# Dilated window attention inside a matmul stream: visits of two pairs of blocks in place of visits of one

## The chip, the cores and the metric

The kernel runs on one core of a Trainium2 chip, in one launch. The metric is the device time of that launch in microseconds (us), the median of several runs. The same work must be done before and after; only its order, its buffers and its waits differ.

## What is computed

The reference is one layer of a decoder trunk over 2048 tokens of width 1024, all in fp32. Cut to what matters here:

```python
h = x * (1.0 + scale) + shift
proj = h @ w_in + b_in        # 1024 -> 8704 columns: q, k, v | z_attn | u_x, g_b, g_c, z_conv | g_A, g_B
for g, (window, dilation) in enumerate(((128, 1), (512, 4), (2048, 16))):
    o_g, lse_g = dilated_window_attention(q_g, k_g, v_g)   # 4 heads of 64 per group, ALiBi bias
o_attn = sum over groups of softmax(lse)_g * o_g
y_attn = (o_attn * silu(z_attn)) @ w_proj_attn
y_conv = (g_b * conv3(g_c * u_x) * silu(z_conv)) @ w_proj_conv
merged = sigmoid(g_A) * y_attn + sigmoid(g_B) * y_conv
x = layer_norm(alpha * x + gate * (merged @ w_out + b_out))
```

Attention is done in blocks of 128 queries of one residue class. A block of group 0 or 1 sees its own 128 keys and, unless it is the first of its class, the 128 before; a block of group 2 sees its own alone. There are 6 tiles `t` (two heads each) of 16 blocks, 96 blocks in all. Of a block the kernel needs the scores, their maximum with the bias, the exponentials and their sum, the probabilities turned round (transposed), and their product with the values.

## The kernel before

**The product stream.** The input projection is a two-level block product in the manner of Strassen and Winograd: for each group of weight tiles (`PLAN`, 68 groups) seven products `p` = 0 to 6 are made of halves of the token axis and of the contraction. Products are numbered n = 7g + p, and this number is the clock of the whole kernel: every engine has its own loop over `m` and each piece of work hangs on some `m`. I call it the slot. A product (`product`, lines 1189 to 1234) is twelve matmuls of 512 columns, four each of high by high (L1224), high by low (L1229) and low by high parts (L1232), since fp32 operands are split in two rounded parts. Slots 14 to 475 are the projection, then come 32 units of the two output projections of the branches (L1356 to L1386), then slots 476 to 531 for the last matmul.

**Banks.** PSUM has eight banks. The four of `acc` serve the products (`bank`, L515): p = 0, 2, 4, 6 of a group build up in one bank on top of each other, `acc[g % 2]`; p = 1 and 5 in another, p = 3 in a third. The sums in between have to be read out before the next product is added on top. So in `product` p = 2 waits until p = 0 has been copied to `part` (semaphore `p1_out`), p = 4 waits for the copy of p = 2 (`u2_out`), p = 6 for the read of p = 4 (`c22_out`). In each of these three only one other product lies between.

**ScalarE (ACT)** in its iteration m (L1636 to L1690, in this order): takes product m-1 where its p is 0, 1 or 2 (`take`, L1505), or p = 6 of the q, k, v and gate groups (`take`, L1509 and L1514), or computes the sigmoid of p = 6 in a `gz` group (`conv_sigmoid(g, 1)`, L1539, which waits for `c12_out`); then the exponentials of a visit (`soften`, L1570, one activation for each of two blocks and two heads); then the copies of turned probabilities (`copy_probs`, L1580); then rounds the weights of slot m+4 (`round_w`, L1488); then, of slot m-2, the sigmoids of the gate groups (L1521), of p = 4 of `gz` (`conv_sigmoid(g, 0)`, L1535) and the first tap of the convolution of `ug` (`first_tap`, L1547). Sigmoid and Exp don't lie in the same table: between them an ACT_TABLE_LOAD runs.

**VectorE (DVE)** in its iteration m: takes product m-1 where its p is 3 to 6, then `take_o` (L1972, attention outputs from PSUM), then `bias_max` (L1961, one tensor_tensor_reduce for each block and head, then L1965), then `combine` (sums of weight tiles), then `split_w` of slot m+3. Most of these go through one helper, L1719.

**Order of groups.** Slots 14 to 62 and 63 to 125 make q, k, v (groups 0 to 17). Groups 18 to 33 alternate `ug` (even) and `gz` (odd), 34 is `za`, 35 to 42 are `gate` (slots 245 to 300). Group 43 (slot 301) is `za` again, 44 to 59 alternate `ug` and `gz`, 60 to 67 are `gate`. In `gz` VectorE's p = 5 step multiplies the convolution's second half by two factors, one of them the sigmoid of ScalarE, before it raises `c12_out`; product p = 1 of the next group and `conv_sigmoid(g, 1)` wait for that.

**Visits.** Attention goes in between the products. `TWO_AT` holds the slots of 48 visits, one for each pair of blocks j: 119, 125 and so on every 6 slots to 287, then 307 to 421. After product n of a visit TensorE multiplies the previous pair's values (`weigh_values`, L1322) and then makes this pair's scores (`scores`, L1289). ScalarE softens at m = n+2, TensorE turns the probabilities after product n+3 (`turn_probs`, L1305), ScalarE copies them at m = n+4. One set of buffers: scores in two banks (`sc_ps`), turned probabilities in `po` and `xb`, outputs in half of `xb`, one `prob` in SBUF.

```python
TURN_P = [at + 3 for at in TWO_AT[:NTWO]]
                    if m - 2 in TWO_AT[:NTWO]:        # ScalarE
                        soften(TWO_AT.index(m - 2))
                    if m - 1 in TWO_AT[:NTWO]:        # VectorE
                        bias_max(TWO_AT.index(m - 1))
```

Of the kernel before, what the change touches and what calls it, by code (L numbers as in the profile page):

```python
# [11 lines left out]
P = 128  # L12
# [122 lines left out]
ATT0 = FIRST[1] + 8 * NP  # L135
NSTEP = NPAIR * NBLK
PAUSE = (FIRST[2] - 9, FIRST[2] + 6)
# [11 lines left out]
SUM_AT = [at + 1 for at in TWO_AT if at >= BG2 + 16][:2]  # L149
# [32 lines left out]
def att_loads(j):  # L182

    return sum({0: 32, NTWO: 16}.get(i, 48) for i in range(j % 2, j + 1, 2))
# [15 lines left out]
def build(nc, x, x_t, c, w_ada_t, w_gate, b_ada, cols_h, w_first, w_tiles, w_pa, w_pc, w_out, b_out, ln_g, ln_b, out):  # L200
# [22 lines left out]
    with ExitStack() as top:  # L223
# [59 lines left out]
        o_ps = xb[:, 0:2 * P]  # L283
# [29 lines left out]
        q_two = view(A, 2, P)  # L313

        k_two = view(A + 256, 3, P)
        v_two = view(A + 640, 3, P)
        dist = view(A + 1024, 2, P)
        bm = view(A + 1280, 2, 2 * P)

        prob = view(A + 1792, 2, 4 * P)  # L320
        prob_t = view(A + 1792, 2, 4 * P)
# [8 lines left out]
        za_s = view(0, 4, CH)  # L330
# [108 lines left out]
        att_in = [sem(f"att_in{r}") for r in range(2)]  # L439
# [213 lines left out]
        with nc.Block() as block:  # L653
            @block.sync
            def _(sp):
# [48 lines left out]
                def load_t(ph, p):  # L704
                    if p == 0:
                        if ph == 1:
                            for idx in (0, 2, 3):
                                sp.wait_ge(hk_out[idx], 16 * KH)
                            sp.wait_ge(tk_out, 16 * 4 * KH)
                        if ph == 2:  # L710
                            for n in ("b11", "b21", "b22", "t1", "t2", "t3", "rest"):
                                sp.wait_ge(dumped[n], 16)
                            sp.wait_ge(gb_out, 16)
                            sp.wait_ge(za_out, 64)
                            for r in range(2):
                                sp.wait_ge(wos_out[r], 16 * 4)
# [7 lines left out]
                def load_att(j):  # L724
                    if j:

                        t, blk = blocks_of(j - 1)
                        first = 0 if has_prev(t, blk) else 1
                        sp.wait_ge(pv_done, j - 1)
                        sp.dma_start(v_two[:, first:3], vt_d[t, blk + first - 1:blk + 2].rearrange("b i f -> i b f")).then_inc(  # L730
                            att_in[j % 2], 16)
                    if j == NTWO:
                        return
# [10 lines left out]
                    if j:  # L744
                        sp.wait_ge(scored, j)
                    first = 0 if has_prev(t, blk) else 1
                    sp.dma_start(q_two.rearrange("p a i -> p (a i)"), qk_d[0, t, :, blk * P:(blk + 2) * P]).then_inc(att_in[j % 2], 16)
                    sp.dma_start(k_two[:, first:3].rearrange("p a i -> p (a i)"),
                                 qk_d[1, t, :, (blk + first - 1) * P:(blk + 2) * P]).then_inc(att_in[j % 2], 16)
# [166 lines left out]
                for m in range(NPAIRED, NS):  # L916
# [9 lines left out]
                    if m + 3 in TWO_AT:  # L926
                        load_att(TWO_AT.index(m + 3))
# [66 lines left out]
            def _(pool):  # L994
# [90 lines left out]
                def store_za(g, n):  # L1085
# [4 lines left out]
                    pool.dma_start(za_d[tile, :, tok], za_s[:, n]).then_inc(za_out, 16)  # L1090
# [25 lines left out]
                for m in range(NPAIRED, NS + 2):  # L1116
# [21 lines left out]
                    if m - 2 in TWO_AT[1:]:  # L1138
                        store_att(TWO_AT.index(m - 2) - 1)
# [42 lines left out]
            def _(pe):  # L1182
# [5 lines left out]
                def product(n):  # L1188
# [6 lines left out]
                    if n in (NS, NS + 1, NS + 3, NS + NP):  # L1195
                        pe.wait_ge(conv_gated, M0 + 4 + {NS: 1, NS + 1: 3, NS + 3: 4, NS + NP: 2}[n])
                    if p == 0:
                        if g >= NG + 2:
                            pe.wait_ge(c21_dve, c21_count(NG - 1, False) + g - NG - 1)
                        elif PLAN[g - 2].kind in C21_ACT:  # L1200
                            pe.wait_ge(c21_act, c21_count(g - 2, True))
                        else:
                            pe.wait_ge(c21_dve, c21_count(g - 2, False))
                        if g == 2:
                            pe.wait_ge(c11_out, 1)
                    if p == 1:
                        pe.wait_ge(c12_out, g)
                    if p == 2:
# [71 lines left out]
                def scores(j):  # L1280
                    t, blk = blocks_of(j)
                    pe.wait_ge(att_in[j % 2], att_loads(j))
                    if j:
                        pe.wait_ge(max_ready, j)
                    for h in range(2):
                        rows_h = slice(h * HEAD, (h + 1) * HEAD)
                        for s in range(2):
                            keys = k_two[rows_h, s:s + 2].rearrange("p a i -> p (a i)") if has_prev(t, blk + s) else k_two[rows_h, s + 1]
                            mm = nc.tensor.matmul(sc_ps[:, h, columns(j, s)], q_two[rows_h, s], keys, start=True, stop=True)  # L1289
                    mm.then_inc(scored, 1)  # L1290

                def turn_probs(j):
                    t, blk = blocks_of(j)
                    pe.wait_ge(exp_done, j + 1)
                    if j:
                        pe.wait_ge(pt_ready, j)
                        pe.wait_ge(o_ready, j)
                    else:
                        pe.wait_ge(v_copied, 4 * len(VG))
                    if TURN_P[j] > SUM_AT[0]:  # L1300
                        pe.wait_ge(gbc_done, sum(TURN_P[j] > at for at in SUM_AT))
                    for s in range(2):
                        for h in range(2):
                            for half in range(0 if has_prev(t, blk + s) else 1, 2):
                                tr = nc.tensor.transpose((po, xb)[s][:, (2 * h + half) * P:(2 * h + half + 1) * P],  # L1305
                                                         prob[:, h, (2 * s + half) * P:(2 * s + half + 1) * P], ident[:])
                    tr.then_inc(turned, 1)

                def weighed(slot):

                    return sum(at <= slot for at in TWO_AT[1:])

                def weigh_values(j):
                    t, blk = blocks_of(j)
                    pe.wait_ge(att_in[(j + 1) % 2], att_loads(j + 1))
                    pe.wait_ge(pt_ready, j + 1)
                    for s in range(2):
                        first = 0 if has_prev(t, blk + s) else 1
                        for h in range(2):
                            cols_h = slice(h * HEAD, (h + 1) * HEAD)  # L1320
                            for half in range(first, 2):
                                mm = nc.tensor.matmul(o_ps[cols_h, s * P:(s + 1) * P], v_two[:, s + half, cols_h],  # L1322
                                                      prob_t[:, s, (2 * h + half) * P:(2 * h + half + 1) * P],
# [3 lines left out]
                def sum_gate(half):  # L1327
# [4 lines left out]
                    nc.tensor.matmul(xb[:], ones[:], gate_acc[:, half * CH:(half + 1) * CH],  # L1332
# [59 lines left out]
                for n in range(NPAIRED, NS):  # L1392
# [3 lines left out]
                    if n in TWO_AT:  # L1396
                        j = TWO_AT.index(n)
                        if j:
# [17 lines left out]
            def _(act):  # L1416
# [106 lines left out]
                def za_sigmoid(g, n):  # L1523
                    sc = PLAN[g].sc
                    if n < 3:
                        act.wait_ge(z1_ready, kind_count(g, "gz") + 3 * sc + n + 1)
                        nc.scalar.activation(za_s[:, n], tmp[:, n], ACT.Sigmoid).then_inc(sig_ready, 1)
# [824 lines left out]
```

## Time and profile before

| what | value |
|---|---|
| median of three runs | 1857.41 us (1857.31 to 1858.83) |
| time of the profiled execution | 1858.69 us |
| its span in the profile | 1856.9 us |
| mean granted TensorE clock | 0.995 |
| TensorE (PE) busy | 1829.5 us, 99% |
| VectorE (DVE) busy | 1241.1 us, 67% |
| ScalarE (ACT) busy | 861.9 us, 46% |
| GpSimd (POOL) busy | 200.5 us, 11% |
| chain that ended last | PE 93%, DMA 2%, DVE 2%, ACT 1%, issue 1% |
| exponentials, L1570 | 192 activations 86.4 us, reads of the sum 35.9 us, 25 table loads 32.1 us |

The span is 1.8 us shorter than the execution's own time; the rest is start and end. A busy time is the union of an engine's instructions. Matmuls overlap each other in the profile, so the steps from one start to the next tell the pace better than durations. An engine's idle time stands in brackets with what released it.

### The profile page before, as it was taken

What the parts mean: (1) busy time and instruction counts of PE and PEld (TensorE: products, weight loads), DVE (VectorE), ACT (ScalarE), POOL (GpSimd) and SP (SyncE); (2) the same over time, 40 slices, a digit from 0 to 9 for tenths busy, and PEclk for the clock granted to TensorE, in tenths of its full rate; (3) what the DMA queues carried; (4) which work ended last, traced back from release to release, by engine and by line L of the source; (5) the groups of instructions that cost most, each with busy time, mean ns of one, the idle gap of its engine ahead of it and who ended that gap; (6) DMA issues with size and microseconds to landing.
All of it is one profiled execution on the core that took longest, in us unless ns stands there. A gap on an engine that the chain in (4) does not pass through costs nothing.

```text
span 1856.9 us, 24751 instructions
## 1 busy us (share of the span) xinstructions
PE 1829.5 (99%) x8783; PEld 1490.7 (80%) x8783; DVE 1241.1 (67%) x2185; ACT 861.9 (46%) x1552; POOL 200.5 (11%) x326
## 2 busy tenths in 40 slices
PE   8999999999999999999999999999999999999997
PEld 7788888888888888877878888888888888887885
DVE  8755744456666666665686666766677576647987
ACT  5544633444555545666665455455444410014342
POOL 0232111100000000011200000000111100011110
PEclk9999999999999999999999999999999999999999
DMA  9876532432232322364862222222396778879782
GB/s 374 291 241 239 188 130 93 117 112 81 94 111 67 109 92 88 129 215 143 299 237 91 94 99 103 80 91 80 118 293 198 257 234 229 249 219 295 206 233 85
DMA packets 161916, 311.27 MB, mean 168 GB/s; under 512 B 35745, under 2 KB 87713, under 8 KB 157570
## 3 DMA queue, kind: packets, MB, share of 16 engines
q1 hardware_dynamic: 132786, 208.64, 34.8%
q0 software_dynamic: 28720, 100.46, 15.8%
q8 instruction: 71, 1.16, 0.3%
q10 hardware_dynamic: 288, 0.59, 0.1%
q14 instruction: 51, 0.42, 0.1%
HBM read 217.06 MB, written 92.57 MB: 167 GB/s over the span
## 4 chain that ended last, share of the span: by engine, by line
PE 93%; DMA 2%; DVE 2%; ACT 1%; issue 1%; SPq 0%; POOL 0%; ACTq 0%; DVEq 0%
PE acc L1224 24%; PE acc L1229 24%; PE acc L1232 24%; PE acc L1378 3%; PE acc L1386 3%; PE acc L1382 3%; PE score L1289 2%; PE xb L1322 2%; PE acc L1240 1%; PE xb L1305 1%; PE pt_o L1305 1%; DMA room<-in_x 1%; DMA vt_d<-room 1%; DVE room L1719 1%; DMA room<-gb_d 1%
## 5 line engine op out<-in xcount | busy, mean ns | idle before, releaser
L1224 PE MATMUL acc<-t_hi,w_hi 128*128 128x512 f32 x1888 | 519.7, 397 | 3.5 <-DVE room L1719 2.2
L1229 PE MATMUL acc<-t_lo,w_hi 128*128 128x512 f32 x1888 | 505.9, 390 | 0.0
L1232 PE MATMUL acc<-t_hi,w_lo 128*128 128x512 f32 x1888 | 505.3, 389 | 0.0
L1229 PEld LDWEIGHTS acc<-t_lo,w_hi 128*128 128x128 f32 x1888 | 354.4, 188 | 75.8
L1232 PEld LDWEIGHTS acc<-t_hi,w_lo 128*128 128x128 f32 x1888 | 354.4, 188 | 75.0
L1224 PEld LDWEIGHTS acc<-t_hi,w_hi 128*128 128x128 f32 x1888 | 344.4, 188 | 84.7 <-issue 14.3
L1719 DVE TENSOR_TENSOR room<-acc,part 128x512 f32<-128x512 f32 x198 | 136.7, 691 | 216.1 <-PE acc L1232 214.4
L1505 ACT ACTIVATE part<-acc,cols 128x512 f32<-128x512 f32 x198 | 136.3, 688 | 211.3 <-PE acc L1232 211.0
L1719 DVE TENSOR_TENSOR w_lo<-w_raw,w_hi 128x512 fp32r<-128x512 f32 x278 | 187.7, 686 | 38.0 <-ACT w_hi L1488 36.6
L1488 ACT CAST w_hi<-w_raw 128x512 fp32r<-128x512 f32 x270 | 166.2, 616 | 99.4 <-PE acc L1232 97.0
L1488 ACT CAST w_hi<-s_tmp 128x512 fp32r<-128x512 f32 x203 | 125.6, 619 | 170.3 <-PE acc L1232 152.5
L1719 DVE TENSOR_TENSOR w_lo<-s_tmp,w_hi 128x512 fp32r<-128x512 f32 x203 | 139.4, 687 | 66.2 <-ACT w_hi L1488 63.8
L1719 DVE TENSOR_TENSOR room<-room 128x512 f32<-128x512 f32 (+2 forms) x208 | 145.4, 703 | 39.0 <-ACT room L1535 30.6
L1570 ACT ACTIVATE room<-room 128x128 f32<-128x128 f32 (+1 forms) x192 | 86.4, 451 | 54.8 <-DVE room L1965 54.6
L1076 POOL DMA_DIRECT2D att_d<-room x48 | 34.4, 717 | 528.7 <-DVE room L1972 528.7
L1719 DVE TENSOR_TENSOR w_raw<-w_raw 128x512 f32<-128x512 f32 x98 | 67.5, 688 | 4.6
L1719 DVE TENSOR_TENSOR s_tmp<-w_raw,s_tmp 128x512 f32<-128x512 f32 x74 | 51.0, 690 | 28.9 <-PE acc L1232 25.9
L1961 DVE CUSTOM_DVE_ANT_0 room<-score,room 128x128 f32<-128x128 f32 (+1 forms) x192 | 58.7, 362 | 16.8 <-PE score L1289 16.5
L1719 DVE TENSOR_TENSOR t_lo<-t_raw,t_hi 128x2048 fp32r<-128x2048 f32 (+1 forms) x29 | 57.6, 1993 | 13.9 <-ACT t_hi L1597 10.2
L1589 ACT CAST t_hi<-t_raw 128x2048 fp32r<-128x2048 f32 x6 | 11.4, 1907 | 112.7 <-DMA t_raw<-conv_d 112.7
L1098 POOL DMA_DIRECT2D gate_d<-room x64 | 34.8, 545 | 239.7 <-ACT room L1521 239.6
L1719 DVE TENSOR_TENSOR s_tmp<-w_raw 128x512 f32<-128x512 f32 x74 | 51.0, 689 | 5.4 <-DMA w_raw<-mix_d 1.1
(257 smaller groups left out, 2087.2 us busy)
## 6 DMA issues: line engine op xcount, KB each, us to landing
w_raw<-in_w_tiles SPq DMA_DIRECT2D x132, 512.0 KB, 4.4
gate_d<-room POOLq DMA_DIRECT2D x64, 256.0 KB, 4.0
qk_d<-room POOLq DMA_DIRECT2D x24, 512.0 KB, 5.1
w_raw<-gate_d SPq DMA_DIRECT2D x24, 512.0 KB, 6.1
room<-qk_d SPq DMA_DIRECT2D x74, 128.0 KB, 3.0
t_raw<-tr_d SPq DMA_DIRECT2D x8, 1024.0 KB, 6.9
conv_d<-room POOLq DMA_DIRECT2D x16, 512.0 KB, 2.9
w_raw<-mix_d SPq DMA_DIRECT2D x16, 512.0 KB, 7.0
```

The lines of the kernel that those rows point to most:

```text
L1224: nc.tensor.matmul(to, hi_w[:, k], hi_t[:, k], start=(first and k == 0), stop=False, skip_group_check=True)
L1229: nc.tensor.matmul(to, hi_w[:, k], lo_t[:, k], start=False, stop=False, skip_group_check=True)
L1232: mm = nc.tensor.matmul(to, lo_w[:, k], hi_t[:, k], start=False, stop=(last and k == KH - 1), skip_group_check=True)
L1289: mm = nc.tensor.matmul(sc_ps[:, h, columns(j, s)], q_two[rows_h, s], keys, start=True, stop=True)
L1378: nc.tensor.matmul(to, w_h[:, k], b_half(True, k), start=(k == 0), stop=False)
L1382: nc.tensor.matmul(to, w_l[:, k], b_half(True, k), start=False, stop=False)
L1386: mm = nc.tensor.matmul(to, w_h[:, k], b_half(False, k), start=False, stop=(k == KT - 1))
L1488: nc.scalar.copy(w_slot(hi_parts, n), src).then_inc(hi_done, 1)
L1505: ins = nc.scalar.activation(to, src, ACT.Identity, bias=col(gr.tb if p == 1 else gr.ta))
L1570: ex = nc.scalar.activation(prob[:, h, o], prob[:, h, o], ACT.Exp, bias=all_m[:, t, h, b], scale=SCALE, accum_out=all_d[:, t, h, b])
L1719: return nc.vector.tensor_tensor(o, a, b, op)
L1961: own_t.up(nc.vector.tensor_tensor_reduce(out=prob[:, h, o], in0=sc_ps[:, h, o], in1=bm[:, h, o.start - 2 * P * s:2 * P], scale=1.0, scala ...
```

## The change

Two pairs of blocks go in one visit, so there are 24 visits (`SCORE_AT`), 35/3 slots apart up to number 13 and 11 apart from number 14 on: 129, 140, 152, 164, 175, 187, 199, 210, 222, 234, 245, 257, 269, 280, then 307, 318, 329, 340, 351, 362, 373, 384, 395, 406. The values are multiplied at the next visit's slot, those of the last before the break at 290 and the very last at 417. ScalarE softens both pairs at m = n+4, TensorE turns both after product n+6, VectorE finds both pairs' maxima at m = n+2. The second pair needs buffers of its own: scores and turned probabilities of a pair share two banks (`att_ps`), the outputs take the fourth bank of `acc`, and so the products get by with three. q, k, v and `prob` are doubled in SBUF, in room that `za_s` and others gave up. In the diff a few lines on addresses, on loads of v and on `za_s` are left out.

```diff
-ATT0 = FIRST[1] + 8 * NP
-PAUSE = (FIRST[2] - 9, FIRST[2] + 6)
-TWO_AT = []
-for j in range(NTWO + 1):
-    slot = TWO_AT[-1] + 6 if j else ATT0
-    TWO_AT.append(PAUSE[1] if PAUSE[0] <= slot < PAUSE[1] else slot)
-TURN_P = [at + 3 for at in TWO_AT[:NTWO]]
-ATT_END = TWO_AT[-1]
+NVISIT = NTWO // 2
+VISIT0 = FIRST[1] + 66
+BREAK = 14
+SCORE_AT = [VISIT0 + 35 * v // 3 if v < BREAK else FIRST[2] + 6 + 11 * (v - BREAK) for v in range(NVISIT)]
+TURN_P = [at + 6 for at in SCORE_AT]
+WEIGH_AT = [SCORE_AT[v + 1] if v + 1 not in (BREAK, NVISIT) else at + (10 if v + 1 == BREAK else 11) for v, at in enumerate(SCORE_AT)]
+ATT_END = WEIGH_AT[-1]
...
-        o_ps = xb[:, 0:2 * P]
+        o_ps = acc[:, 3]
+        att_ps = ((sc_ps[:, 0], sc_ps[:, 1]), (po[:], xb[:]))
...
+        prob = (view(0, 2, 4 * P), view(2 * CH, 2, 4 * P))
+        prob_t = prob
...
         def bank(g, p):
-            if p in (0, 2, 4, 6):
-                return acc[:, g % 2]
-            return acc[:, 2] if p in (1, 5) else acc[:, 3]
+            if p in (1, 5):
+                return acc[:, 1]
+            return acc[:, 2 * ((g + (p == 3)) % 2)]
...
                             sp.wait_ge(za_out, 64)
+                            sp.wait_ge(pv_done, 2 * BREAK)
...
                     if p == 0:
-                        if g >= NG + 2:
-                            pe.wait_ge(c21_dve, c21_count(NG - 1, False) + g - NG - 1)
-                        elif PLAN[g - 2].kind in C21_ACT:
-                            pe.wait_ge(c21_act, c21_count(g - 2, True))
-                        else:
-                            pe.wait_ge(c21_dve, c21_count(g - 2, False))
-                        if g == 2:
-                            pe.wait_ge(c11_out, 1)
+                        pe.wait_ge(c11_out, 1 if g == 2 else g)
...
                     if p == 3:
-                        pe.wait_ge(c11_out, g)
-                        if g == 2:
-                            pe.wait_ge(c22_out, 1)
+                        if g > NG:
+                            pe.wait_ge(c21_dve, c21_count(NG - 1, False) + g - NG)
+                        elif PLAN[g - 1].kind in C21_ACT:
+                            pe.wait_ge(c21_act, c21_count(g - 1, True))
+                        else:
+                            pe.wait_ge(c21_dve, c21_count(g - 1, False))
...
                 def scores(j):
                     t, blk = blocks_of(j)
-                    pe.wait_ge(att_in[j % 2], att_loads(j))
-                    if j:
-                        pe.wait_ge(max_ready, j)
+                    u = j % 2
+                    if u == 0:
+                        pe.wait_ge(qk_in, 64 * (j // 2 + 1))
+                        if j:
+                            pe.wait_ge(pt_ready, j)
+                        else:
+                            pe.wait_ge(v_copied, 4 * len(VG))
...
-                    if n in TWO_AT:
-                        j = TWO_AT.index(n)
-                        if j:
-                            weigh_values(j - 1)
-                        if j < NTWO:
+                    if n in WEIGH_AT:
+                        for j in pair(WEIGH_AT.index(n)):
+                            weigh_values(j)
+                    if n in SCORE_AT:
+                        for j in pair(SCORE_AT.index(n)):
                             scores(j)
                     if n in TURN_P:
-                        turn_probs(TURN_P.index(n))
+                        for j in pair(TURN_P.index(n)):
+                            turn_probs(j)
...
-                    if m - 2 in TWO_AT[:NTWO]:
-                        soften(TWO_AT.index(m - 2))
+                    if m - 4 in SCORE_AT:
+                        for j in pair(SCORE_AT.index(m - 4)):
+                            soften(j)
                     if m - 1 in TURN_P:
-                        copy_probs(TURN_P.index(m - 1))
+                        for j in pair(TURN_P.index(m - 1)):
+                            copy_probs(j)
...
-                    if m - 1 in TWO_AT[1:]:
-                        take_o(TWO_AT.index(m - 1) - 1)
-                    if m - 1 in TWO_AT[:NTWO]:
-                        bias_max(TWO_AT.index(m - 1))
+                    if m - 1 in WEIGH_AT:
+                        for j in pair(WEIGH_AT.index(m - 1)):
+                            take_o(j)
+                    if m - 2 in SCORE_AT:
+                        for j in pair(SCORE_AT.index(m - 2)):
+                            bias_max(j)
```

## Rows read from the trace of the kernel before

**Rows 1.** The page, part 1: busy time and share of the span

```profile
PE 1829.5 (99%) x8783; PEld 1490.7 (80%) x8783; DVE 1241.1 (67%) x2185; ACT 861.9 (46%) x1552; POOL 200.5 (11%) x326
```

**Rows 2.** Waits, TensorE: us in total, times, longest us

```profile
PE acc L1224 <- ACT part L1505: 1.1, 1, 1.1
```

**Rows 3.** Timeline of TensorE around the visit at slot 161: start, us, instructions

```profile
499.46 0.39 PE L1232 MATMUL acc<-t_hi,w_lo 128*128 128x512 f32 x1
499.77 1.14 PE L1322 MATMUL xb<-room 128*64 128x128 f32 x16
...
500.65 0.27 PE L1322 MATMUL xb<-room 128*64 128x128 f32 x1
500.85 0.49 PE L1289 MATMUL score<-room 64*128 64x256 f32 x2
...
501.17 0.60 PE L1289 MATMUL score<-room 64*128 64x256 f32 x4
501.38 0.60 PE L1289 MATMUL score<-room 64*128 64x256 f32 x4
...
501.92 1.19 PE L1224 MATMUL acc<-t_hi,w_hi 128*128 128x512 f32 x4
502.95 1.08 PE L1229 MATMUL acc<-t_lo,w_hi 128*128 128x512 f32 x4
```

**Rows 4.** Timeline of TensorE, slots 259 to 261: the one wait for ScalarE

```profile
815.29 1.07 PE L1224 MATMUL acc<-t_hi,w_hi 128*128 128x512 f32 x4
...
818.01 1.07 PE L1224 MATMUL acc<-t_hi,w_hi 128*128 128x512 f32 x4
...
820.73 0.60 PE L1305 MATMUL pt_o<-ident,room 128*128 128x128 f32 x4
...
822.83 1.15 PE L1224 MATMUL acc<-t_hi,w_hi 128*128 128x512 f32 x4 [1.06 <-ACT part L1505]
```

**Rows 5.** Timeline of ScalarE in the same stretch

```profile
815.49 0.69 ACT L1514 ACTIVATE room<-acc,cols 128x512 f32<-128x512 f32 x1 [3.69 <-PE acc L1232]
816.28 1.28 ACT L1570 ACT_TABLE_LOAD   x1
817.57 0.51 ACT L1570 ACTIVATE room<-room 128x256 f32<-128x256 f32 x1
...
819.56 0.60 ACT L1488 CAST w_hi<-w_raw 128x512 fp32r<-128x512 f32 x1
...
822.01 0.67 ACT L1505 ACTIVATE part<-acc,cols 128x512 f32<-128x512 f32 x1
```

**Rows 6.** Timeline of ScalarE, slots 161 to 171: first tap, sigmoids, exponentials of a pair

```profile
500.98 1.15 ACT L1547 ACTIVATE room<-room,cols 128x1024 f32<-128x1024 f32 x1
...
520.93 0.69 ACT L1539 ACTIVATE room<-acc,cols 128x512 f32<-128x512 f32 x1 [1.54 <-DVE room L1719]
...
524.36 0.69 ACT L1505 ACTIVATE part<-acc,cols 128x512 f32<-128x512 f32 x1 [2.24 <-PE acc L1232]
525.07 1.28 ACT L1570 ACT_TABLE_LOAD   x1
526.37 0.40 ACT L1570 ACTIVATE room<-room 128x128 f32<-128x128 f32 x1
...
528.13 0.60 ACT L1488 CAST w_hi<-s_tmp 128x512 fp32r<-128x512 f32 x1
528.64 0.68 ACT L1505 ACTIVATE part<-acc,cols 128x512 f32<-128x512 f32 x1
```

**Rows 7.** Timeline of VectorE, slots 161 to 167: maxima of a pair, then a gz group

```profile
502.05 0.43 DVE L1961 CUSTOM_DVE_ANT_0 room<-score,room 128x256 f32<-128x256 f32 x1 [0.67 <-PE score L1289]
...
503.63 0.69 DVE L1719 TENSOR_TENSOR w_lo<-w_raw,w_hi 128x512 fp32r<-128x512 f32 x1
...
514.04 0.69 DVE L1719 TENSOR_TENSOR room<-acc,part 128x512 f32<-128x512 f32 x1 [0.92 <-PE acc L1232]
514.88 0.69 DVE L1719 TENSOR_TENSOR w_raw<-w_raw 128x512 f32<-128x512 f32 x1
...
519.41 1.42 DVE L1719 TENSOR_TENSOR room<-room 128x512 f32<-128x512 f32 x2 [1.23 <-ACT room L1535]
```

**Rows 8.** Timeline of TensorE in the last matmul, after a longer wait

```profile
1705.41 2.04 PE L1224 MATMUL acc<-w_hi,t_hi 128*128 128x512 f32 x4 [2.34 <-DVE sums_y L2109]
...
1709.71 1.08 PE L1224 MATMUL acc<-t_hi 128*128 128x512 f32 x4
```

**Rows 9.** Stretches: busy of PE, PEld, DVE, ACT, POOL, then PEclk, DMA share, GB/s

```profile
820.00:830.00 10.00, 8.94 (x44) 7.32 (x44) 6.47 (x9) 7.05 (x12) 1.80 (x3) 1.00 0.48 162
1705.00:1709.00 4.00, 3.59 (x9) 2.87 (x10) 2.88 (x8) 1.55 (x3) 1.76 (x3) 0.57 1.17 286
```

More of the change, by code:

```diff
@@ L179, in columns, with pair @@
     return slice(2 * P * s + (0 if has_prev(t, blk + s) else P), 2 * P * (s + 1))
-def att_loads(j):
-    return sum({0: 32, NTWO: 16}.get(i, 48) for i in range(j % 2, j + 1, 2))
+def pair(v):
+    return 2 * v, 2 * v + 1
 class Tally:
@@ L312, in build @@
         A = 2048
[L313 to L321, printed above, removed]
+        q_two = view(A, 2, 2, P)
+        k_two = view(A + 512, 2, 3, P)
+        v_two = view(A + 1280, 2, 3, P)
+        dist = view(A + 2048, 2, P)
+        bm = view(A + 2304, 2, 2 * P)
+        prob = (view(0, 2, 4 * P), view(2 * CH, 2, 4 * P))
+        prob_t = prob
         att_o = view(A + 2816, 2, 2 * P)
@@ L329, in build @@
         tmp3 = view(ROOM - 4 * CH, CH)
-        za_s = view(0, 4, CH)
+        za_s = [view(first, CH) for first in (6916, 6916 + CH, 8964, 8964 + CH)]
         gate_w = view(5888, 2, D)
@@ L438, in build @@
         dist_done = sem("dist_done")
-        att_in = [sem(f"att_in{r}") for r in range(2)]
+        qk_in = sem("qk_in")
+        v_in = sem("v_in")
         scored = sem("scored")
@@ L722, in load_t, with load_qk @@
                     sp.dma_start(dst, tr_d[(0, 1, 0)[ph], p]).then_inc(t_in[p % 4], 16)
-                def load_att(j):
-                    if j:
[L727 to L733, printed above, removed]
+                def load_qk(j):
                     t, blk = blocks_of(j)
@@ L925, in _ @@
                                 load_t(ph, p)
-                    if m + 3 in TWO_AT:
-                        load_att(TWO_AT.index(m + 3))
+                    if m + 4 in SCORE_AT:
+                        for j in pair(SCORE_AT.index(m + 4)):
+                            load_qk(j)
+                    if m - 2 in SCORE_AT:
+                        for j in pair(SCORE_AT.index(m - 2)):
+                            load_v(j)
                     for k in range(KT + 1):
@@ L1137, in _ @@
                         make_dist()
-                    if m - 2 in TWO_AT[1:]:
-                        store_att(TWO_AT.index(m - 2) - 1)
+                    if m - 2 in WEIGH_AT:
+                        for j in pair(WEIGH_AT.index(m - 2)):
+                            store_att(j)
                     if m == BG2 + 29:
@@ L1293, in turn_probs @@
                     t, blk = blocks_of(j)
+                    u = j % 2
                     pe.wait_ge(exp_done, j + 1)
[L1295 to L1301, printed above, removed]
                     for s in range(2):
@@ L1304, in turn_probs @@
                             for half in range(0 if has_prev(t, blk + s) else 1, 2):
-                                tr = nc.tensor.transpose((po, xb)[s][:, (2 * h + half) * P:(2 * h + half + 1) * P],
-                                                         prob[:, h, (2 * s + half) * P:(2 * s + half + 1) * P], ident[:])
+                                tr = nc.tensor.transpose(att_ps[u][s][:, (2 * h + half) * P:(2 * h + half + 1) * P],
+                                                         prob[u][:, h, (2 * s + half) * P:(2 * s + half + 1) * P], ident[:])
                     tr.then_inc(turned, 1)
                 def weighed(slot):
-                    return sum(at <= slot for at in TWO_AT[1:])
+                    return 2 * sum(at <= slot for at in WEIGH_AT)
                 def weigh_values(j):
                     t, blk = blocks_of(j)
-                    pe.wait_ge(att_in[(j + 1) % 2], att_loads(j + 1))
+                    u = j % 2
+                    if u == 0:
+                        pe.wait_ge(v_in, 32 * (j // 2 + 1))
+                        if j:
+                            pe.wait_ge(o_ready, j)
+                        if WEIGH_AT[j // 2] > SUM_AT[0]:
+                            pe.wait_ge(gbc_done, 2)
                     pe.wait_ge(pt_ready, j + 1)
@@ L1331, in sum_gate @@
                     pe.wait_ge(o_ready, weighed(SUM_AT[half]))
-                    nc.tensor.matmul(xb[:], ones[:], gate_acc[:, half * CH:(half + 1) * CH],
+                    nc.tensor.matmul(o_ps, ones[:], gate_acc[:, half * CH:(half + 1) * CH],
                                      start=True, stop=True).then_inc(gsum, 1)
@@ L1578, in copy_probs @@
                         first = 0 if has_prev(t, blk + s) else P
-                        to = prob_t[:, s].rearrange("p (h n) -> p h n", h=2)
-                        ins = nc.scalar.copy(to[:, :, first:], (po, xb)[s][:].rearrange("p (h n) -> p h n", h=2)[:, :, first:])
+                        to = prob_t[j % 2][:, s].rearrange("p (h n) -> p h n", h=2)
+                        ins = nc.scalar.copy(to[:, :, first:], att_ps[j % 2][s].rearrange("p (h n) -> p h n", h=2)[:, :, first:])
                     ins.then_inc(pt_ready, 1)
@@ L1910, in take_za @@
                         dve.wait_ge(sig_ready, sig + 4)
-                        nc.vector.scalar_tensor_tensor(out=za_s[:, 3], in0=bank(g, 6), scalar=col(gr.tb), in1=za_s[:, 3],
+                        nc.vector.scalar_tensor_tensor(out=za_s[3], in0=bank(g, 6), scalar=col(gr.tb), in1=za_s[3],
                                                        op0=ALU.add, op1=ALU.mult).then_inc(c21_dve, 1)
@@ L1961, in bias_max @@
                             own_t.up(nc.vector.tensor_tensor_reduce(
-                                out=prob[:, h, o], in0=sc_ps[:, h, o], in1=bm[:, h, o.start - 2 * P * s:2 * P], scale=1.0,
+                                out=prob[j % 2][:, h, o], in0=att_ps[j % 2][h][:, o], in1=bm[:, h, o.start - 2 * P * s:2 * P], scale=1.0,
                                 scalar=-3.0e38, op0=ALU.add, op1=ALU.max, accum_out=all_m[:, t, h, blk + s:blk + s + 1]))
```

62 lines of the change are left out of this document (39 added, 23 removed).

## The prediction

> **What bounds the kernel now.** I read the page's busy times first: TensorE is busy for 99% of the span, VectorE for 67%, ScalarE for 46% [rows 1]. So only two things can move the end: what TensorE executes, and the time in which it is made to wait. The view of waits says that in the whole product stream ScalarE made it wait once, for 1.1 us [rows 2]. Then I read the timeline of TensorE through one visit, to see what a visit costs beyond its matmuls [rows 3], and the timelines of ScalarE and VectorE where a visit falls on a product whose bank must be read at once [rows 4 to 7].
>
> **The pace.** A product takes 2.72 us, 815.29 to 818.01 [rows 4], 0.227 us a matmul. ScalarE's copy starts 0.20 us after its product ends (815.29 to 815.49), and TensorE goes on 0.15 us after that copy ends (822.01 + 0.67 = 822.68, then 822.83) [rows 4, 5]. p = 2 adds on p = 0 with one product between, p = 4 on p = 2 likewise. So from the end of the product that is read before, ScalarE's work up to the copy's end has 5.44 us less 0.15.
>
> **Part 1, half the visits: a gain.** In the visit at slot 161 the last product matmul starts at 499.46 and the values at 499.77: 0.31 instead of 0.23, 0.08 lost. The values' records step by 0.06 (499.77 to 500.65 is 15 steps of 0.88), but the step to the scores is 0.20: 0.14 lost. Scores go in pairs of records: 0.32 for the first pair, 0.21 for the second, 0.54 for the last two with the way out, against 0.21 a pair: 0.11 and 0.12 lost. The first four product matmuls take 1.03 instead of 0.91 [rows 3]: 0.12. That is 0.57, say 0.6 us, in each visit whatever its size. 24 visits less give 14.4 us; the break now separates values and scores at one more place, which takes 0.2 back: **-14.2 us**. Turning probabilities has almost no such cost (eight transposes in the 0.9 us that they take at any place); I take 0, between 0 and -1. The matmuls themselves are the same.
>
> **Part 2, both pairs' exponentials in one step: a cost.** ScalarE needs 1.99 us for a full pair (817.57 to 819.56) [rows 5], 1.76 where one block has no predecessor (526.37 to 528.13) [rows 6], so some 1.53 where both have none. One pair, with its table load, between two copies takes 4.96 us, start of the first to end of the second (524.36 to 528.64 + 0.68) [rows 6]. With 0.20 and 0.15 around it that is 5.3 of 5.44 us: it just fits. A second pair doesn't. Softening is at m = n+4, behind the copy of product n+3 and ahead of that of n+4, so it bites where n+4 has p = 0 or 2.
> - n with p = 5 (152, 187, 222, 257, 362; n+4 is p = 2): 4.96 + 0.23 + 1.99 + 0.35 = 7.5 us for two full pairs, 2.1 over; 1.9 with a mixed pair (257), about 1.2 with pairs of group 2 (362). At 152, 187, 222 VectorE makes it worse: its two maxima (1.58 us each, 502.05 to 503.63 [rows 7], 3.2 together) stand behind its work on p = 6, done about 2.3 us after that product, and ahead of the `combine` (0.6) that the rounding just before ScalarE's copy of p = 1 needs. That rounding ends at 2.3 + 3.2 + 0.6 + 0.5 = 6.6 instead of by 5.64: 1.0 more, 3.1 each. Together 3 x 3.1 + 1.9 + 1.2 = 12.4 us.
> - n with p = 3 in a `gz` group (164, 234, 318; n+4 is p = 0): before the exponentials stands the sigmoid that waits for VectorE's `c12_out`. VectorE reads p = 4 and goes on 0.84 later (514.04, 514.88 [rows 7]), then 3.2 of maxima, 1.2 for two helper steps, then four steps for p = 5, 2.8: 8.3 after p = 4 ends, which is 2.9 after p = 6. In rows 6 the sigmoid starts at 520.93, about 1.6 after p = 6. From it again 7.2, and 0.15: 10.3 against 5.44, 4.8 over; 4.3 with a mixed pair. Together 13.4.
> - n with p = 3 in a `gate` group (269): here the trace shows the case itself with one pair. From the end of p = 6 to the start of p = 2 it takes 7.54 us (815.29 to 822.83 [rows 4, 5]); a second, mixed pair makes 9.3: 3.9 over.
> - smaller: 340 (n+4 is p = 1, but exponentials, rounding and the first tap of 1.15 [rows 6] reach the copy of p = 2) 0.8, and 373, where the maxima stand ahead of the read of p = 4, 0.4.
> The sum is 12.4 + 13.4 + 3.9 + 1.2 = **+30.9 us**. Elsewhere the copy comes before the exponentials, or none is due; `ug` groups with n at p = 3 have no step of ScalarE that waits for p = 6, so they start early. The wait of rows 4 goes: the transposes' start to 822.83 is 2.1 us where 0.9 is needed, **-1.2**.
>
> By the Trainium skill, ScalarE: Activation LUTs, What ACT_TABLE_LOAD costs, a switch is the load of 1.283 us and a drain of about 1.38. The rows show the load at 816.28 and the first exponential at 817.57, so no drain here [rows 5]. With the drain ten of the chains above would be an estimated 14 us longer; the row excludes it, so it gets no chance of its own.
>
> **Part 3, the clock.** After the 2.34 us wait the next twelve matmuls took 4.30 us instead of 2.72 [rows 8], and the granted clock of that stretch is 0.57, the lower level of 1.2 GHz in most of it, where the stretch after a 1.06 us wait keeps 1.00 [rows 9]. The three of 3.1, the three of `gz` and the gate one are longer than 2.34: 7 x 1.6 = **+11.2 us**. Bounds: nothing, and twice that.
>
> **Part 4, what costs nothing.** Three banks for the products: p = 3 now waits for p = 6 of the group before, p = 0 for p = 3, with three products (8.2 us) between, more than any chain above; bound 0 to +2. Copies of two pairs stand behind the copies of products: 0. The doubled loads run two and more slots ahead of their use, and SyncE's new wait before the restart at 291 delays the 1 MB loads by the 2 us of one visit: 0, bound +2. Fewer table loads help only ScalarE's total.
>
> **Sum.** -14.2 - 1.2 + 30.9 + 11.2 = +26.7 us. The profiled execution has a span of 1856.9 and a time of 1858.7, 1.3 over the median of 1857.4; on the median it gives **1884 us**.
>
> **Rivals.**
> - *Faster.* The fixed cost goes and no wait takes its place: 1857.4 - 15.4 = 1842 us. Its place is the copy of p = 0 or p = 2 behind `soften`, its price each wait above, and it decides where the chain from the product's end stays under 5.29 us. For it speak ScalarE's 54% of idle time and that 13 of the 24 visits have no such chain. Against it that one pair already takes 5.3, or 7.54 in a gate group. It also turns faster if the waits come to under 15 us with the clock kept. Chance 0.15.
> - *The waits come, the clock stays.* 1857.4 - 15.4 + 30.9 = 1873 us. For it: a wait of 1.06 left the clock at 1.00; only one longer wait is in the rows. Chance 0.22.
> - *Half the waits.* If VectorE's share (the 1.0 and 1.3 parts) and the short ones don't appear, some 15 to 20 us of waits are left and a few drops: 1860 us. Chance 0.13.
> - *More waits*, or each drop of the clock twice as dear: 26.7 + 11.2 over, 1895 us and more. Chance 0.10.
> - The forecast: 0.40.
>
> **Numbers.** 0.2% or 3.7 us is what a measurement tells from no change. The forecast, the second rival and the last are slower; half the waits is slower or the same. Faster 0.15, same 0.05, slower 0.80. The range goes from 1860, which leaves out the faster case, to 1897.
>
> **What would show it.** TensorE's waits for ScalarE (L1224 after `part` L1505) should rise from one of 1.1 us to about ten with 25 to 30 us in all, at products n+6 of the visits named; longest at 170, 240, 324 and 275. After them steps of 0.43 us. The start-to-start costs of a visit of twice the size should be 0.6 us under two old ones. VectorE would show no wait at p = 3. Wrong it is if the list of waits stays at 1 or 2 us, if they stand at p = 0, 1 or 3 (banks), or if the clock stays at 1.00.

## The result, and the profile after

The changed kernel takes 1896.59 us (median of four, 1895.37 to 1897.13), against 1858.12 of the kernel before on the same chip. The ratio is 1.0202, with a 95% interval of 1.0189 to 1.0215. It is slower by 38.5 us. I had forecast 1884, 26.7 us slower, in a range of 1860 to 1897: the measured time lies 0.4 us under the upper end.

The profiled execution of the changed kernel has a span of 1894.8 us. The page's busy times, to be held against [rows 1]:

```profile
PE 1831.4 (97%) x8783; PEld 1504.4 (79%) x8783; DVE 1236.0 (65%) x2185; ACT 849.1 (45%) x1544; POOL 200.0 (11%) x326
```

TensorE executes the same 8783 matmuls and is busy 2 us longer, in a span 38 us longer. That looks as if all the new time were waiting, but two parts cancel in it: slower matmuls and cheaper visits (the account below has both). The view of waits of TensorE, where [rows 2] had one of 1.1 us for ScalarE:

```profile
PE acc L1224 <- ACT part L1511: 27.9, 9, 4.2
PE acc L1224 <- DVE room L1731: 8.9, 7, 5.3
PE acc L1240 <- ACT t_hi L1451: 3.8, 1, 3.8
...
PE acc L1224 <- DVE part L1731: 1.0, 1, 1.0
```

L1511 is the copy to `part` (L1505 before). It now makes TensorE wait nine times. One of them is at slot 158, after the visit at 152. The timeline of TensorE there, then that of ScalarE, and that of VectorE just before:

```profile
485.94 1.28 PE L1224 MATMUL acc<-t_hi,w_hi 128*128 128x512 f32 x4 [3.07 <-ACT part L1511]
487.02 1.91 PE L1229 MATMUL acc<-t_lo,w_hi 128*128 128x512 f32 x4
488.72 1.79 PE L1232 MATMUL acc<-t_hi,w_lo 128*128 128x512 f32 x4
```

```profile
478.13 0.62 ACT L1494 CAST w_hi<-s_tmp 128x512 fp32r<-128x512 f32 x1 [2.69 <-DVE s_tmp L1731]
478.66 0.69 ACT L1511 ACTIVATE part<-acc,cols 128x512 f32<-128x512 f32 x1
479.36 1.28 ACT L1580 ACT_TABLE_LOAD   x1
480.66 0.51 ACT L1580 ACTIVATE room<-room 128x256 f32<-128x256 f32 x1
...
484.61 0.60 ACT L1494 CAST w_hi<-w_raw 128x512 fp32r<-128x512 f32 x1
485.12 0.68 ACT L1511 ACTIVATE part<-acc,cols 128x512 f32<-128x512 f32 x1
```

```profile
474.22 0.41 DVE L1975 CUSTOM_DVE_ANT_0 room<-score,room 128x256 f32<-128x256 f32 x1
...
477.41 0.69 DVE L1731 TENSOR_TENSOR s_tmp<-w_raw,s_tmp 128x512 f32<-128x512 f32 x1
```

The chain is the predicted one, link for link. VectorE's maxima of both pairs take 474.22 to 477.41, and its `combine` stands behind them. ScalarE waits for that `combine` (2.69 us, of which a part is its ordinary waiting), copies p = 1 late, loads the table, runs eight exponentials for 3.95 us (480.66 to 484.61), and only then copies p = 2, which ends at 485.80. TensorE starts p = 4 at 485.94.

The `gz` form is at slot 170, after the visit at 164: the sigmoid at 523.77 waits for VectorE, then come the load and eight exponentials, and the copy of p = 0 starts at 530.23. The view names TensorE as what ended that wait, but p = 6 had ended at 520.8; what ends just before 523.77 is VectorE's work on p = 5, at 523.68.

```profile
523.77 0.69 ACT L1547 ACTIVATE room<-acc,cols 128x512 f32<-128x512 f32 x1 [2.56 <-PE acc L1232]
524.48 1.28 ACT L1580 ACT_TABLE_LOAD   x1
...
529.72 0.60 ACT L1494 CAST w_hi<-w_raw 128x512 fp32r<-128x512 f32 x1
530.23 0.68 ACT L1511 ACTIVATE part<-acc,cols 128x512 f32<-128x512 f32 x1
```

```profile
521.66 2.02 DVE L1731 TENSOR_TENSOR room<-room 128x512 f32<-128x512 f32 x3
```

TensorE resumes at 531.05, its longest wait of this kind (4.23 us). Measured in the timeline, from the start at which each product would have followed the one before, the waits against the forecast are:

| slot of the wait | forecast | measured |
|---|---|---|
| 158, 193, 228 | 3.1 each | 3.2, 3.1, 3.3 |
| 170, 240, 324 | 4.8, 4.3, 4.3 | 4.4, 4.2, 4.2 |
| 275 | 3.9 | 3.8 |
| 263, 368 | 1.9, 1.2 | 1.8, 1.3 |
| 347 (visit at 340) | 0.8 | none |
| 377, 379 | 0.4 | 0.8, 0.9 |
| sum | 30.9 | 31.1 |
| 433 | not foreseen | 5.5 |

**The clock.** Stretches of 4 us after three of the waits; the columns are those of rows 9:

```profile
486.00:490.00 4.00, 4.00 (x11) 3.09 (x12) 1.75 (x4) 0.82 (x2) 0.00 (x0) 0.60 0.76 253
531.00:535.00 4.00, 3.95 (x10) 3.13 (x11) 2.03 (x4) 1.51 (x3) 0.00 (x0) 0.57 0.07 20
849.00:853.00 4.00, 3.67 (x20) 3.13 (x21) 3.85 (x6) 1.22 (x3) 0.00 (x0) 1.00 0.58 200
```

After the waits of 3.1 and 4.4 us the granted clock is 0.60 and 0.57, so in most of the stretch it is the lower level, 1.2 GHz; after the 1.8 us at slot 263 it is 1.00. In the product stream of this kernel there are eight waits of 3.1 us and more, the seven above and the one at 433, and all eight were followed by such a stretch.

**A visit.** Slot 164, values and scores of two full pairs:

```profile
507.54 1.07 PE L1232 MATMUL acc<-t_hi,w_lo 128*128 128x512 f32 x4
508.54 2.02 PE L1327 MATMUL acc<-room 128*64 128x128 f32 x32
510.49 1.14 PE L1294 MATMUL score<-room 64*128 64x256 f32 x8
...
512.52 1.19 PE L1224 MATMUL acc<-t_hi,w_hi 128*128 128x512 f32 x4
513.55 0.62 PE L1229 MATMUL acc<-t_lo,w_hi 128*128 128x512 f32 x2
```

From 507.54 to 513.55 are 6.01 us. Eight product matmuls at the ordinary pace are 1.81, so the visit costs 4.20. In [rows 3] the same reckoning, 499.46 to 502.95 less five steps, gives 2.36, and twice that is 4.72. The gain is 0.52 us, not 0.6.

**The wait at 433**, for VectorE's read of p = 4 in group 61. The timeline of SyncE shows its cause:

```profile
1358.97 11.80 SPq L780 DMA_DIRECT2D room<-stat_d  x24
1370.81 2.36 SPq L658 DMA_DIRECT2D w_raw<-in_w_tiles  x2
1373.27 0.52 SPq L867 DMA_DIRECT2D room<-wos_d  x1
```

```profile
1379.41 0.62 ACT L1494 CAST w_hi<-w_raw 128x512 fp32r<-128x512 f32 x1 [4.14 <-DMA w_raw<-in_w_tiles]
```

```profile
1382.36 2.87 DVE L1731 TENSOR_TENSOR room<-room 128x512 f32<-128x512 f32 x4 [1.65 <-DMA room<-wos_d]
1385.15 0.68 DVE L1731 TENSOR_TENSOR room<-acc,part 128x512 f32<-128x512 f32 x1
...
1387.19 0.68 DVE L1731 TENSOR_TENSOR room<-acc,part 128x512 f32<-128x512 f32 x1
```

```profile
1388.02 2.05 PE L1224 MATMUL acc<-t_hi,w_hi 128*128 128x512 f32 x4 [5.31 <-DVE room L1731]
```

Attention ends at slot 417 instead of 421, and `STAT`, `WEIGH` and `WQ_AT` hang on `ATT_END`. So the 24 small loads of the statistics, 11.8 us of issuing, moved from slot 426 to 422, and the weights of group 62, issued at slot 423, now stand behind them. ScalarE waits 4.14 us for those weights. VectorE reaches the read of p = 3 at 1385.15, after the sums of w_out, which had to wait for a load behind the same queue, and the read of p = 4 at 1387.19; TensorE waited from 1382.55 to 1388.02.

**The account**, in us of span: start of the kernel +1.6 (a transfer of v lands later, see below); visits -12.1 and turning (the transposes) -0.4; the wait at 261 gone -1.3; waits of the chains +31.1; slower matmuls after eight drops of the clock +14.2; wait at 433 less one of 0.4 before +5.1; last matmul -0.5, what follows it +0.3. Sum +38.0; the spans differ by 37.9.

### The profile page after: what moved, and what is told of

It is laid out like the page before. It is cut to its first block, busy times and chain, and to the rows that moved or that the text cites. A ratio compares the mean times of both kernels' runs of the same rounds, so it can differ in the third digit from the quotient of the medians.

```text
span 1894.8 us, 24637 instructions
## 1 busy us (share of the span) xinstructions
PE 1831.4 (97%) x8783; PEld 1504.4 (79%) x8783; DVE 1236.0 (65%) x2185; ACT 849.1 (45%) x1544; POOL 200.0 (11%) x326
## 4 chain that ended last, share of the span: by engine, by line
PE 86%; DVE 4%; ACT 4%; DMA 3%; issue 2%; SPq 0%; POOL 0%; ACTq 0%; DVEq 0%
PE acc L1224 22%; PE acc L1229 22%; PE acc L1232 22%; PE acc L1383 3%; PE acc L1391 3%; PE acc L1387 3%; PE acc L1327 2%; ACT room L1580 2%; DVE room L1731 1%; PE acc L1240 1%; DVE room L1975 1%; PE score L1294 1%; PE score L1304 1%; DMA vt_d<-room 1%; DMA room<-in_x 1%
## 5 line engine op out<-in xcount | busy, mean ns | idle before, releaser
L1224 PE MATMUL acc<-t_hi,w_hi 128*128 128x512 f32 x1888 | 521.0, 398 | 38.1 <-ACT part L1511 27.9
L1224 PEld LDWEIGHTS acc<-t_hi,w_hi 128*128 128x128 f32 x1888 | 349.8, 189 | 121.3 <-ACT w_hi L1494 36.6
L1229 PEld LDWEIGHTS acc<-t_lo,w_hi 128*128 128x128 f32 x1888 | 358.3, 190 | 76.6
L1511 ACT ACTIVATE part<-acc,cols 128x512 f32<-128x512 f32 x198 | 136.4, 689 | 232.8 <-PE acc L1232 232.3
L1731 DVE TENSOR_TENSOR s_tmp<-s_tmp,w_raw 128x512 f32<-128x512 f32 x74 | 50.7, 685 | 2.2
```

Of the source, the lines that this page charges most:

```text
L1224: nc.tensor.matmul(to, hi_w[:, k], hi_t[:, k], start=(first and k == 0), stop=False, skip_group_check=True)
L1229: nc.tensor.matmul(to, hi_w[:, k], lo_t[:, k], start=False, stop=False, skip_group_check=True)
L1511: ins = nc.scalar.activation(to, src, ACT.Identity, bias=col(gr.tb if p == 1 else gr.ta))
L1731: return nc.vector.tensor_tensor(o, a, b, op)
```

## Experiments

Each ran beside the kernel before on the same chip; differences are between medians. The changed kernel itself was not run again with them: a difference from it is taken to its 1896.59, which stood beside 1858.1 of the kernel before, where the experiments stood beside 1859.1 and 1859.2. So such a difference is good to about 1 us.

**The second pair's exponentials one iteration later.** This undoes one part of the change, "both pairs in one step", on ScalarE alone.

```diff
-                    if m - 4 in SCORE_AT:
-                        for j in pair(SCORE_AT.index(m - 4)):
-                            soften(j)
+                    for u in range(2):
+                        if m - 4 - u in SCORE_AT:
+                            soften(2 * SCORE_AT.index(m - 4 - u) + u)
```

> The first pair's exponentials stay in ScalarE's iteration n+4, the second pair's go to n+5. Theory (both pairs in one ScalarE iteration stand before a copy that TensorE needs): at visits with p = 5 one pair and its table load fit, so the waits at products 158, 193, 228, 263 and 368 shrink by 2 us each (from 3.2, 3.1, 3.3, 1.8, 1.3), those at 170, 240, 324 and 275 from 4.1 to 4.4 down to 2.1 to 2.4, and some clock drops go with them: 9 waits x 2 us and 3 to 5 drops x 1.5, so 20 to 25 us less than the changed kernel, 1872 to 1877. Rival (what holds TensorE is VectorE's later maxima or the three banks): no change, 1896.

Measured: 1869.86 us (1866.92 to 1871.07), ratio to the kernel before 1.0058 (1.0043 to 1.0073). That is 26.7 less than the changed kernel, a little more than the upper end of what I expected. The waits for ScalarE:

```profile
PE acc L1224 <- ACT part L1511: 11.8, 8, 2.3
PE acc L1224 <- DVE room L1731: 8.1, 5, 5.5
```

27.9 us became 11.8. At 158, 193 and 228 waits of 1.2 to 1.3 are left, at 170, 240 and 324 2.2 to 2.4, and 263 and 368 have none. Five of seven drops of the clock in the attention stretch are gone. The step of two pairs is the cause of most of the loss. What is left at 158, 193 and 228 is of the size of VectorE's share, as the run on the maxima below shows; at 170, 240, 324, and at 275 with 1.9, more is left than that share, and no run takes it apart.

**The later work back in its slots.**

```diff
-ATT_END = WEIGH_AT[-1]
+ATT_END = WEIGH_AT[-1] + 4
```

> The work that follows attention (statistics, their loads, the sums of w_out) is put back to the slots it had before the change, 4 later. Theory: the wait of 5.3 us at product 433 comes from the 24 small loads of the statistics, now issued by SyncE just ahead of the weights of group 62; it goes with its clock drop, so 7 us less than the changed kernel, 1889 to 1890, and ScalarE no longer waits 4.1 us for w_raw there. Rival (the wait comes from the three banks or from contention of the transfers): it stays, 1896.

Measured: 1889.27 us (1888.42 to 1889.39), ratio 1.0164 (1.0149 to 1.0179), 7.3 less than the changed kernel. The wait at 433 is gone: the longest for VectorE is 1.2 us.

```profile
PE acc L1224 <- ACT part L1511: 27.9, 9, 4.3
...
PE acc L1224 <- DVE room L1731: 3.4, 6, 1.2
```

The statistics are issued behind the weights of slot 423 again:

```profile
1353.43 0.86 SPq L658 DMA_DIRECT2D w_raw<-in_w_tiles  x2
1359.64 0.38 SPq L867 DMA_DIRECT2D room<-wos_d  x1
1366.59 14.09 SPq L780 DMA_DIRECT2D room<-stat_d  x24
```

In the changed kernel's timeline the wait at 433 and the slow matmuls behind it are 5.5 and 1.7 us, and that is what this run takes away. That its time fell by just as much has some luck in it: v's transfer at the start landed 1.2 us sooner here, the clock fell after the wait at 482 (1.6 us) and not after the one at 228 (1.6), two other drops were 1.1 and 1.3 us dearer and one 0.8 cheaper, and these cancel. The run moves all the later work by four slots; that it is the order of the loads in the queue that matters is read from the timelines. The waits for ScalarE stay what they were, so the two causes are separate.

**Three banks alone.** The kernel before, with the new `bank` and the waits that go with it, as they stand in the change's diff, and nothing else.

> The kernel before with nothing but the new assignment of the products to three banks, and its waits. Theory (a product's bank is free three products ahead of its reuse): same as the kernel before within 0.1%, 1856 to 1860, TensorE's waits unchanged. Rival (the banks cost a share of the 12 us by which the changed kernel is slower than I summed up): 1862 to 1870, with new waits at p = 0 or 3.

Measured: 1858.99 us (1856.9 to 1860.17, ten runs) against 1859.1, ratio 0.9997 (0.9988 to 1.0007). The banks cost nothing, as Part 4 had it, within 0.1%.

**The first pair's maxima one iteration earlier.**

```diff
-                    if m - 2 in SCORE_AT:
-                        for j in pair(SCORE_AT.index(m - 2)):
-                            bias_max(j)
+                    for u in range(2):
+                        if m - 1 - u in SCORE_AT:
+                            bias_max(2 * SCORE_AT.index(m - 1 - u) + u)
```

> The first pair's maxima move to VectorE's iteration n+1, the second's stay at n+2; ScalarE's step of two pairs is as in the changed kernel. Theory: VectorE's two maxima in one step delay what comes before ScalarE's chain by 1.0 to 1.3 us at six of the visits (152, 187, 222 by the combine, 164, 234, 318 by the factor behind c12_out); half of that or more goes, 4 to 7 us less than the changed kernel, 1889 to 1893, with the waits at 158, 193, 228 near 2.2. Rival (VectorE has no share, ScalarE's chain alone sets the waits): 1896, waits unchanged. Against me: maxima now stand ahead of the read of p = 4 where n has p = 3, which can make TensorE wait at p = 6.

Measured: 1884.76 us (1882.99 to 1885.9), ratio 1.0138 (1.0123 to 1.0153): 11.8 less, where I had expected 4 to 7. The waits at 158 and 193 are 2.05, at 228 1.8, at 170 3.8, at 240 and 324 3.3, and those at 377 and 379 are gone: 8.0 us in all. Three drops of the clock go too, with the waits that fell from over 3 to 2 us. VectorE's share was placed right. Its size is 1.1 to 1.5 us at 158, 193 and 228, where Part 2 had 1.0, and 0.6 to 0.9 at 170, 240 and 324, where it had 1.3. What this run gained beyond my expectation is the clock and the waits at 377 and 379, which I had left out. The wait at 275, to which VectorE contributes nothing by Part 2, stays at 3.85.

**No table switch.** The exponential is left out: Sigmoid is computed in its place, with the same activations.

```diff
-                            ex = nc.scalar.activation(prob[j % 2][:, h, o], prob[j % 2][:, h, o], ACT.Exp, bias=all_m[:, t, h, b],
+                            ex = nc.scalar.activation(prob[j % 2][:, h, o], prob[j % 2][:, h, o], ACT.Sigmoid, bias=all_m[:, t, h, b],
```

> Leaves out the exponential: the same activations run with Sigmoid in its place, so that no table is loaded between them and the other sigmoids; all else as in the changed kernel. Theory: each of the nine ScalarE waits is shorter by its table load of 1.28 us, that of 275 by two; waits for ScalarE fall from 27.9 to about 15, most clock drops of the shorter ones go, so 12 us of waits and 4 to 7 of clock less than the changed kernel, 1877 to 1881. Rival (the loads run while ScalarE would be idle anyway): 1894 or more. If a switch also cost a drain, the waits would fall by twice as much.

Measured: 1870.01 us (1869.11 to 1871.41), ratio 1.0058 (1.0041 to 1.0075): 26.6 less. The waits behaved as expected:

```profile
PE acc L1224 <- ACT part L1511: 14.2, 8, 2.8
```

They are 14.2, against "about 15"; the waits at 158, 193, 170, 240 and 324 are 1.4 each shorter, the one at 275 2.7 (two switches). The activations themselves step by 0.49 us with either function. So a switch costs its load of 1.28 and about 0.1, and no drain. The time fell by 7 to 11 us more than I expected, though. The slow matmul steps, 55 in the changed kernel and 23 here, give 6.4 of the gain, which is within the 4 to 7 that I had for the clock. Of what I hadn't expected 2.9 us lie before slot 119: the copy of v, which waited long for a transfer in the changed kernel, didn't in this run (1.4), and the first product started 0.9 us sooner. Another 1.7 are waits for ScalarE, 13.7 less where I had 12. The rest is not placed.

**The same steps at other slots.** Both pairs still go in one step on every engine. Only the slots change: all visits but the first lie where p = 0, so that softening (n+4) follows the copy of p = 2, and the next copy is due after p = 6.

```diff
-SCORE_AT = [VISIT0 + 35 * v // 3 if v < BREAK else FIRST[2] + 6 + 11 * (v - BREAK) for v in range(NVISIT)]
+SCORE_AT = ([129] + [140 + 35 * k + x for k in range(4) for x in (0, 14, 21)] + [280] +
+            [FIRST[2] + 7 + 21 * k + x for k in range(5) for x in (0, 14)])
...
-ATT_END = WEIGH_AT[-1]
+ATT_END = WEIGH_AT[-1] + 4
...
-SUM_AT = (BG2 + 18, BG2 + 20)
+SUM_AT = (BG2 + 21, BG2 + 23)
```

> The changed kernel with all visits but the first at slots where p = 0 (14, 7 and 14 apart), so that the exponentials of both pairs stand behind the copy of p = 2 and before no other; the later work as in e2; the two sums of the gate 3 slots later. Nothing else differs: both pairs still go in one step on each engine. Theory: nearly all waits for ScalarE go (under 3 us in all), no clock drop in the attention stretch, and the gain of fewer visits (0.5 us each, 12 us) is what is left: 1845 to 1849, below the kernel before. Rival (any ScalarE step of two pairs is too long wherever it lies, or visits 7 slots apart make TensorE wait for the copies): 1860 or more.

Measured: 1843.71 us (1843.11 to 1845.07), ratio to the kernel before 0.9921 (0.9906 to 0.9936). It is 52.9 us faster than the changed kernel and 15.4 faster than the one before, so it beats both, and it lies 1.3 us under the range that I expected. In its view of waits no row has ScalarE's copy to `part` any more:

```profile
PE xb L1278 <- ACT room L1573: 3.2, 3, 1.2
PE acc L1241 <- ACT t_hi L1452: 3.2, 1, 3.2
PE acc L1225 <- DVE room L1732: 3.1, 5, 1.2
PE acc L1225 <- DVE sums_y L2124: 2.3, 1, 2.3
```

ScalarE after the visit at slot 154: its exponentials run until 509.20, then it rounds, and has idle time before the next thing that is due.

```profile
508.70 0.50 ACT L1581 ACTIVATE room<-room 128x256 f32<-128x256 f32 x1
509.10 0.19 ACT L1581 ACTIVATION_READ_ACCUMULATOR room<-room 128x1 f32 x1
509.20 1.13 ACT L1495 CAST w_hi<-s_tmp 128x512 fp32r<-128x512 f32 x2
512.37 0.62 ACT L1495 CAST w_hi<-w_raw 128x512 fp32r<-128x512 f32 x1 [2.04 <-PE acc L1233]
```

The exponentials take as long as in the changed kernel; nobody waits for them. The visits cost TensorE the same as there (82.8 us in both, 94.9 in the kernel before), so this run also measures the gain of Part 1 by itself. Of its span, 14.6 us shorter than the one before, 12.1 are the visits, 0.4 the turning, 1.3 the old wait and 1.6 the clock, which didn't fall after the wait of 2.3 us in the last matmul; 1.5 are lost again at the start, on the copy of v named below. The first product starts 0.8 us sooner, which a wait at slot 485 takes back. That leaves 0.7 unplaced.

## Why the prediction was right, and where it was short

- **Part 2, the waits**, 30.9 forecast, 31.1 measured, and nine of the ten places I priced over 0.5 us are right to 0.4 us. The split of the exponentials, the run without table loads and the other slots each took away the share that the chain gives them; the split of the maxima did so to within 0.1 to 0.5 us at 158, 193 and 228, and took 0.4 to 0.7 less than I had at 170, 240 and 324. The one place that failed is 347, after the visit at 340: there p = 4 waits for nothing. At 377 and 379 I had 0.4 and it is 1.7.
- **Part 3, the clock.** I had 7 drops at 1.6 us, 11.2. There were these seven and an eighth after the wait at 433, and all eight cost 14.2, so 1.8 each. The price came from one wait, with seven slow steps behind it; one of the new stretches had twelve (after the wait at 240).
- **Part 1, the gain**, was mis-sized: 14.2 forecast, 12.5 measured with the turning. The step failed that summed what looked lost within a visit. Of the 0.23 us that I put down to the scores only 0.11 were saved: one pair's scores take 1.07 us, 500.85 to 501.92 [rows 3], and two pairs' take 2.03, 510.49 to 512.52. The values saved 0.21, 0.07 more than I had (2 x 1.08 against 1.95 us, 508.54 to 510.49), and rounding 0.57 up to 0.6 took 0.7 us over all visits.
- **Part 4, what costs nothing**, is where the largest miss lies. The banks are right (0.9997). The list left out that `ATT_END` moves everything that hangs on it. The row to read was there in the kernel before, whose SyncE timeline shows the 24 loads taking 12.8 us to issue; I hadn't asked which slot of `load_w` they would now precede. It cost 5.5 us of waiting and 1.7 of clock, and both are gone in the run that puts them back.

```profile
1337.45 12.79 SPq L783 DMA_DIRECT2D room<-stat_d  x24
```

- **The price of a table switch.** The rule of the Trainium skill (ScalarE: Activation LUTs, What ACT_TABLE_LOAD costs) that adds a drain of about 1.38 us doesn't hold in this kernel: without the loads each chain became 1.4 us shorter per switch, not 2.7.
- **The rivals.** "Faster" needed ScalarE's chain under 5.29 us, and with waits of 1.3 to 4.4 it was 6.6 to 9.7. "The waits come, the clock stays" fell with eight drops, and "half the waits" with 31.1 us of them. "More waits" had 1895 us and more, and by the time alone it is what came. Its mechanism is in part there too: one wait that I had not foreseen, and drops a tenth dearer, not twice.
- **The size of the miss.** The spans differ by 37.9 us, 11.2 more than I forecast: the wait at 433 with its slow matmuls is 6.8 of it, the gain 1.7, the start 1.6, the seven other drops 1.3. So the mechanism that I described came as described, but nothing in my sum allowed for the wait at 433; that the time still fell inside the range, by 0.4 us, is luck. The part at the start, 1.6 us, was not foreseen either: the third copy of v waited 2.60 us for an earlier transfer of v to land, 1.21 in the kernel before. It is there in the changed kernel and in three of the five experiments made from it, and missing in two, which are the same up to there (the later work put back, and no table switch). What makes that transfer late was not tried.

## What to carry to other kernels

Two steps merged into one on an engine that is half idle can still stop the bounding engine: what counts is not the engine's share but the longest run of work that it puts ahead of something due soon, and where in the period that run falls. Find the gap between a product and the read that its successor needs, subtract what already stands in it, and place the merged step in a phase where nothing is due; the same code at other slots was worth 45.6 us here beyond the 7.3 of putting the later work back. And when a change moves the end of a phase, follow every slot that is defined by that end, through each DMA queue.

## What the runs showed of the hardware that I had not expected

- The length of a wait alone does not tell whether the clock falls. All 8 waits of 3.1 us and more in the changed kernel's product stream were followed by matmuls at about 0.43 us a step; waits of 2.05 and less never were, in the product stream of any of these runs. Between them it goes both ways, and even 3.3 us decide nothing: the wait at slot 228 was 3.3 us long in the changed kernel and with the later work back in its slots, and was followed by a granted clock of 0.68 in the first and of 1.00 in the second (first two rows below). With the exponentials in two steps the wait of 2.2 us at slot 324 was followed by a granted clock of 0.57 in a 4 us stretch, while after one of 2.4 us at slot 170 it stayed at 1.00 (last two rows); and the 2.3 us wait for `sums_y` in the last matmul, the same in all kernels, was followed by slow matmuls in the kernel before and not in the changed one.

```profile
727.70:731.70 4.00, 4.00 (x13) 3.06 (x14) 1.80 (x4) 0.88 (x2) 0.00 (x0) 0.68 0.72 258
727.60:731.60 4.00, 4.00 (x24) 3.46 (x25) 2.80 (x6) 1.22 (x4) 0.00 (x0) 1.00 0.74 266
1025.00:1029.00 4.00, 3.53 (x9) 2.86 (x10) 1.53 (x3) 3.89 (x12) 0.00 (x0) 0.57 0.24 99
524.00:529.00 5.00, 4.07 (x24) 3.54 (x25) 2.29 (x4) 5.00 (x15) 0.00 (x0) 1.00 0.11 47
```

- A TensorE visit between products of another shape costs about 0.5 us on top of its matmuls, and as much with two pairs as with one: 4.20 against 2 x 2.36 us for full pairs, 2.43 against 2 x 1.46 for pairs without predecessors.
